# Expert units of 128 rows in a mixture-of-experts stage: rows stationary, gate and up columns moving in one product, hidden values turned by TensorE, down product one group later

## The chip, the cores and the metric

The program runs on one core of one Trainium2 chip. The metric is the device time of one execution in microseconds (us), lower is better. The kernel is a two-block transformer; the change touches one part of it, the expert stage, which takes some 17% of the time.

## What is computed

The reference has many stages; only the expert feed-forward matters here. 512 tokens with 1024 features each pick 2 of 8 experts, and each expert runs a SwiGLU with 3584 hidden columns on the rows that picked it:

```python
top_logits, top_idx = lax.top_k(logits, TOP_K)
...
order = jnp.argsort(flat_e)
group_sizes = jnp.bincount(flat_e, length=N_EXPERTS).astype(jnp.int32)
xs = xt[order // TOP_K]
hid = (jax.nn.silu(lax.ragged_dot(xs, w_gate, group_sizes))
       * lax.ragged_dot(xs, w_up, group_sizes))
ys = lax.ragged_dot(hid, w_down, group_sizes)
```

All of it is in float32. The weights of one expert (gate, up and down, 1024 x 3584 each) do not fit on the chip with everything else, so they are streamed from memory, and every unit of rows streams all of its expert's weights.

## The kernel before

`experts_stage` works through units. A unit is one expert's rows: at most 128 rows (units A, `ExpertRows` size 0) or at most 152 (units B, size 1). With these inputs there are five units A, then three units B. The 3584 hidden columns are cut into 14 groups of 256 (`GROUP`), and two sets of weight tiles alternate (index `b`, the group's parity). A float32 product of TensorE stands in the trace as two passes (two MATMUL rows, each with its own weight load), so the counts of the trace are twice those of the code.

In a unit A, for each group TensorE runs `first_half` (L1893): twice (`j`, 128 hidden columns each) `gate_up` (L1885), which takes 8 blocks of gate weights as stationary operand with the 128 turned rows `xu` moving, then 8 blocks of up weights. That gives gate and up values with hidden columns on the partitions, in banks 4 and 5 (gate), 6 and 7 (up). ScalarE applies Silu (L1983) to `gs`, VectorE multiplies (L2013) into `hid`. Then `down_a` (L1898) multiplies `hid` (stationary, 128 x 128, two of them) by the down weights (moving, 512 columns) and adds into banks 0 and 1, which hold the unit's output rows. In what follows P(g) is the gate and up product of group g and D(g) its down product. The order on TensorE before is P(0) D(0) P(1) D(1) ... P(13), the turning of the next unit's rows (`turn`, L1815, 8 transposes), D(13).

The weights come by DMAs that SyncE issues in a fixed order, for each group: wait until the gate and up tiles of this parity are free (`freed[b]`), issue gate (L1868) and up (L1869), wait until the down tile of this parity is free (`down_freed[b]`), issue down (L1875). 1 MiB each. `freed[b]` is incremented by the first matmul of D(g), `down_freed[b]` by the last one of D(g). P(g) waits for `loaded[b]`, that is for both gate and up. All three go through SyncE's one queue.

At the end of a unit VectorE copies the output from banks 0 and 1 (L2030), ScalarE's queue stores it (L1831), and GpSimd fetches the rows of the unit after the next one's turn (L1799 the indices, L1803 the rows, 512 KB).

Of the kernel before, what the change touches and what calls it, by code (L numbers as in the profile page):

```python
# [14 lines left out]
F32 = mybir.dt.float32  # L15
# [3 lines left out]
ALU = mybir.AluOpType  # L19
ACT = mybir.ActivationFunctionType  # L20
AX = mybir.AxisListType

P = 128
# [3 lines left out]
KD = D // P  # L27
# [7 lines left out]
GROUP = 256  # L35
# [125 lines left out]
class Stages:  # L161
# [10 lines left out]
    def sig(self, name, pool_dma=False):  # L172

        if name not in self.signals:
            self.signals[name] = Signal(self.nc, self.stack, name, True) if pool_dma else self.spare.pop()
        return self.signals[name]
# [11 lines left out]
def settle(eng, passed):  # L188


    eng.sem_inc(passed.sem, 1)
# [1573 lines left out]
class ExpertRows:  # L1765


    def __init__(self, S, R, size, st):
        self.S, self.R = S, R
        self.unfetched = 1 if size == 0 else 0  # L1770
        self.rows, self.row0 = UNIT_ROWS[size], FIRST_ROW[size]
        self.subs = [(r0, min(P, self.rows - r0)) for r0 in range(0, self.rows, P)]
        self.bank0 = (2, 4)[size]
        n = len(self.subs)
        self.xg = S.sb(f"rows{size}_x", [P, n, D], F32, st)
        self.xu = S.sb(f"rows{size}_xt", [P, KD, self.rows], F32, st)
        self.yrow = S.sb(f"rows{size}_y", [P, n, D], F32, st)
        self.index = S.sb(f"rows{size}_index", [P, n], I32, st)
        self.indexed, self.gathered = (S.sig(f"e{size}_{x}", pool_dma=True) for x in ("indexed", "gathered"))
        self.turned, self.stored, self.x_ready = (S.sig(f"e{size}_{x}") for x in ("turned", "stored", "x_ready"))  # L1780
        sig = lambda x: S.sig(f"s{size}_{x}")
        self.loaded, self.freed = [sig("loaded0"), sig("loaded1")], [sig("freed0"), sig("freed1")]
        self.down_loaded, self.down_freed = [sig("down_loaded0"), sig("down_loaded1")], [sig("down_freed0"), sig("down_freed1")]
        self.hidden, self.gate_up, self.gated = ([sig(x + "0"), sig(x + "1")] for x in ("hidden", "gate_up", "gated"))
        self.y_taken = sig("y_taken")
        if size:
            self.y_ready, self.y_turned, self.emitted = sig("y_ready"), sig("y_turned"), sig("emitted")

    def units(self, eng):
        size = 0 if self.row0 == 0 else 1  # L1790
# [43 lines left out]
def experts_stage(S, R, router, xn):  # L1834
    nc, a, ps = S.nc, S.a, S.ps
    n_groups = E_FF // GROUP
    per = n_groups // 2
    zeros = S.sig("s1_zeros")
    last = n_groups - 1
    with ExitStack() as st:  # L1840
        wg = S.sb("experts_wg", [P, 2, KD, GROUP], F32, st)
        wu = S.sb("experts_wu", [P, 2, KD, GROUP], F32, st)
        wd = S.sb("experts_wd", [P, 2, 2, D], F32, st)
        gs = S.sb("experts_gs", [P, 2, UNIT_ROWS[1]], F32, st)
        hid = S.sb("experts_hid", [P, 2, UNIT_ROWS[1]], F32, st)
        yT = S.sb("experts_yt", [P, KD, UNIT_ROWS[1]], F32, st)
        zero = S.sb("experts_zero", [P, BANK], BF16, st)
        A, B = ExpertRows(S, R, 0, st), ExpertRows(S, R, 1, st)
# [3 lines left out]
        with nc.Block("experts") as block:  # L1852
# [32 lines left out]
            def _(pe):  # L1885
# [8 lines left out]
                def first_half(E, b, u, i, n):  # L1894
                    pe.wait_ge(E.loaded[b].sem, E.loaded[b].at((u * per + i + 1) * 32))
                    gate_up(E, b, n, 0)
                    gate_up(E, b, n, 1)

                def down_a(b, u, i, n, first=False, final=False):
                    for j in range(2):  # L1900
                        pe.wait_ge(A.hidden[j].sem, A.hidden[j].at(n + 1))
                        if first and j == 0:
                            pe.wait_ge(A.y_taken.sem, A.y_taken.at(u))
                        if j == 0:
                            pe.wait_ge(A.down_loaded[b].sem, A.down_loaded[b].at((u * per + i + 1) * 16))
                        for hf in range(2):
                            ins = nc.tensor.matmul(ps[hf][:, :], hid[:, j, 0:P], wd[:, b, j, hf * 512:(hf + 1) * 512],  # L1907
                                                   start=(first and j == 0), stop=(final and j == 1), skip_group_check=True)
                            if j == 0 and hf == 0:
                                ins.then_inc(A.freed[b].sem, 1)  # L1910
                    ins.then_inc(A.down_freed[b].sem, 1)

                def down_b(b, u, i, n):
# [14 lines left out]
                n_a, n_b = A.units(pe), B.units(pe)  # L1928
                router.first_unit(pe, xn, A.bank0, A.turned)
                with pe.Fori(0, n_a) as u:  # L1930
                    pe.wait_ge(A.x_ready.sem, A.x_ready.at(2 * u + 2))
                    settle(pe, S.sig("passed_pe"))
                    n0 = u * n_groups
                    first_half(A, 0, u, 0, n0)
                    down_a(0, u, 0, n0, first=True)
                    with pe.Fori(0, per - 1) as i:
                        first_half(A, 1, u, i, n0 + i * 2 + 1)
                        down_a(1, u, i, n0 + i * 2 + 1)
                        first_half(A, 0, u, i + 1, n0 + i * 2 + 2)
                        down_a(0, u, i + 1, n0 + i * 2 + 2)  # L1940
                    first_half(A, 1, u, per - 1, n0 + last)
                    A.turn(pe, u + 1)
                    down_a(1, u, per - 1, n0 + last, final=True)
                B.turn(pe, 0)
                pe.wait_ge(A.y_taken.sem, A.y_taken.at(n_a))
                pe.wait_ge(A.x_ready.sem, A.x_ready.at(2 * n_a + 2))
# [2 lines left out]
                with pe.Fori(0, n_b) as u:  # L1949
                    pe.wait_ge(B.x_ready.sem, B.x_ready.at(4 * u + 4))  # L1950
                    settle(pe, S.sig("passed_pe"))
                    n0 = u * n_groups
# [24 lines left out]
            @block.scalar  # L1977
            def _(act):
                def silu(E, u, g, j):
                    n = u * n_groups + g  # L1980
                    act.wait_ge(E.gate_up[j].sem, E.gate_up[j].at(n + 1))
                    act.wait_ge(E.hidden[j].sem, E.hidden[j].at(n))
                    nc.scalar.activation(gs[:, j, 0:E.rows], ps[4 + j][:, 0:E.rows], ACT.Silu).then_inc(E.gated[j].sem, 1)  # L1983

                router.weigh(act)
                act.wait_ge(routed.sem, routed.at(2))
                n_a, n_b = A.units(act), B.units(act)
                with act.Fori(0, n_a) as u:
                    for g in range(n_groups):
                        silu(A, u, g, 0)  # L1990
                        silu(A, u, g, 1)
                    act.wait_ge(A.y_taken.sem, A.y_taken.at(u + 1))
                    settle(act, S.sig("passed_act"))
                    A.store(act, u)
                act.wait_ge(A.hidden[0].sem, A.hidden[0].at(n_a * n_groups))
                act.wait_ge(A.hidden[1].sem, A.hidden[1].at(n_a * n_groups))
                settle(act, S.sig("passed_act"))
                with act.Fori(0, n_b) as u:
                    for g in range(n_groups):
                        silu(B, u, g, 0)  # L2000
                        silu(B, u, g, 1)
                    act.wait_ge(B.emitted.sem, B.emitted.at(4 * u + 4))
                    settle(act, S.sig("passed_act"))
                    B.store(act, u)
                act.wait_ge(A.stored.sem, A.stored.at(16 * n_a))
                act.wait_ge(B.stored.sem, B.stored.at(32 * n_b))
                settle(act, S.sig("passed_act"))

            @block.vector
            def _(dve):  # L2010
                def hidden(E, u, g, j):
                    dve.wait_ge(E.gated[j].sem, E.gated[j].at(u * n_groups + g + 1))
                    nc.vector.tensor_tensor(hid[:, j, 0:E.rows], gs[:, j, 0:E.rows], ps[6 + j][:, 0:E.rows],  # L2013
                                            ALU.mult).then_inc(E.hidden[j].sem, 1)
# [4 lines left out]
                n_a, n_b = A.units(dve), B.units(dve)  # L2019
                A.place(dve, 0)  # L2020
                with dve.Fori(0, n_a) as u:
                    for g in range(n_groups):
                        hidden(A, u, g, 0)
                        hidden(A, u, g, 1)
                    A.place(dve, u + 1)
                    dve.wait_ge(A.down_freed[1].sem, A.down_freed[1].at(u * per + per))
                    dve.wait_ge(A.stored.sem, A.stored.at(16 * u))
                    settle(dve, S.sig("passed_dve"))
                    for hf in range(2):
                        ins = nc.vector.tensor_copy(A.yrow[:, 0, hf * 512:(hf + 1) * 512], ps[hf][:, :])  # L2030
                    ins.then_inc(A.y_taken.sem, 1)
# [1759 lines left out]
```

## Time and profile before

| | |
|---|---|
| median of 3 runs | 4344.17 us (4343.14 to 4347.41) |
| the profiled execution | 4342.29 us |
| its span in the profile | 4340.6 us |
| TensorE busy over the whole span | 3774.5 us (87%) |
| stage of units A | about 1303 to 2071 us |
| stage of units B | about 2071 to 2610 us |

PE is TensorE's matmuls and PEld its weight loads, DVE is VectorE, ACT ScalarE, POOL GpSimd; SPq, ACTq and POOLq are what these engines issue, DMAs among it. Times are from the span's start. A row of the timeline merges instructions of one line that follow each other; the length of a merged row includes the tail of its last matmul, so the distance between the starts of two rows tells what the first one costs TensorE.

### The profile page before, as it was taken

The numbers are of one execution on the slowest core, as the hardware profiler recorded it, in microseconds if no ns is written. First come the engines' busy times: TensorE is split into PE (matmuls) and PEld (weight loads), VectorE is DVE, ScalarE is ACT, GpSimd is POOL, SyncE is SP. The second block draws the span as 40 slices with busy tenths as digits, with TensorE's granted clock in tenths as the row PEclk, the third lists the DMA queues.
The fourth block names the chain that finished last, engine by engine and source line by source line (L and its number), as shares of the span: only waits on it lengthen the run. The fifth ranks groups of instructions, "written<-read, shape, count | busy, mean of one in ns | idle before, by whom it ended". The sixth has DMA issues, their size and how long they took to land. (4 is left out here: it accounts for less than half of the span.)

```text
span 4340.6 us, 45502 instructions
## 1 busy us (share of the span) xinstructions
PE 3774.5 (87%) x17099; PEld 2506.2 (58%) x17106; DVE 1706.2 (39%) x3683; ACT 626.4 (14%) x1566; POOL 1094.1 (25%) x1162
## 2 busy tenths in 40 slices
PE   7989999998988999999999996998766767766666
PEld 3455777744747888888999993465422322222222
DVE  2052231013730000000000004748888776877655
ACT  1121000013520000000000003143211111111011
POOL 0010000001500000000000000003667777777775
PEclk9989999999989999999999998989888888888888
DMA  3143675330018889888777764036899999999998
GB/s 114 48 152 122 240 246 191 105 136 1 20 59 267 307 294 311 306 306 298 264 248 256 252 223 140 25 103 234 336 390 387 419 416 420 413 418 415 420 414 354
DMA packets 549127, 1092.57 MB, mean 252 GB/s; under 512 B 37577, under 2 KB 336982, under 8 KB 548870
## 3 DMA queue, kind: packets, MB, share of 16 engines
q1 hardware_dynamic: 395802, 539.66, 36.8%
q0 software_dynamic: 150768, 546.25, 31.3%
q10 hardware_dynamic: 2428, 5.03, 0.3%
q8 instruction: 69, 1.13, 0.1%
q14 instruction: 60, 0.49, 0.0%
HBM read 1069.55 MB, written 21.30 MB: 251 GB/s over the span
## 5 line engine op out<-in xcount | busy, mean ns | idle before, releaser
L3223 PE MATMUL banks<-peer_ring,consts 128*128 128x512 f32 x1512 | 844.7, 719 | 375.9 <-DMA peer_ring<-in_peer_v_dram,peer_expert 375.9
L3223 PEld LDWEIGHTS banks<-peer_ring,consts 128*128 128x128 f32 x1512 | 338.1, 231 | 877.2 <-DMA peer_ring<-in_peer_v_dram,peer_expert 469.4
L3424 DVE SCALAR_TENSOR_TENSOR peer_ring<-peer_ring,banks 128x1024 f32<-128x1024 f32 x512 | 594.0, 1216 | 253.2 <-DMA peer_ring<-in_peer_u_dram,peer_expert 252.2
L3127 POOL DMA_INDIRECT peer_ring<-in_peer_u_dram,peer_expert x512 | 483.7, 945 | 547.6 <-POOLq L2744 348.0
L3127 POOL DMA_INDIRECT peer_ring<-in_peer_v_dram,peer_expert x512 | 487.4, 952 | 173.5 <-issue 138.5
L2013 DVE TENSOR_TENSOR experts_hid<-experts_gs,banks 128x128 f32<-128x128 f32 (+1 forms) x224 | 66.5, 297 | 1175.8 <-ACT experts_gs L1983 1175.8
L1890 PEld LDWEIGHTS banks<-rows_xt,experts_wg 128*128 128x128 f32 x3584 | 447.0, 192 | 45.2 <-issue 44.9
L1890 PE MATMUL banks<-rows_xt,experts_wg 128*128 128x128 f32 (+1 forms) x3584 | 462.4, 283 | 11.4 <-DMA experts_wu<-in_moe_w_up_dram 9.4
L1890 PE MATMUL banks<-rows_xt,experts_wu 128*128 128x128 f32 (+1 forms) x3584 | 461.1, 282 | 0.0
L1890 PEld LDWEIGHTS banks<-rows_xt,experts_wu 128*128 128x128 f32 x3584 | 441.0, 192 | 0.0
L405 PE MATMUL banks<-xT,proj_w 128*128 128x512 f32 (+1 forms) x720 | 319.3, 601 | 9.0 <-PEq L3575 5.5
L1799 POOL DMA_DIRECT2D rows_index<-token_of_row x13 | 7.4, 575 | 1060.3 <-PE banks L1815 1042.4
L1907 PE MATMUL banks<-experts_wd,experts_hid 128*128 128x512 f32 x560 | 251.9, 593 | 0.0
L405 PEld LDWEIGHTS banks<-xT,proj_w 128*128 128x128 f32 (+1 forms) x720 | 135.6, 191 | 185.3 <-issue 184.0
L1023 POOL TENSOR_TENSOR hgrn_both<-k,hgrn_diff 128x256 f32<-128x256 f32 x56 | 44.3, 815 | 775.6 <-ACT hgrn_diff L934 761.2
L1983 ACT ACTIVATE experts_gs<-banks 128x128 f32<-128x128 f32 (+1 forms) x224 | 63.7, 285 | 1183.0 <-PE banks L1890 1183.0
L3455 DVE SCALAR_TENSOR_TENSOR banks<-peer_ring,peer_wgt,banks 128x1024 f32<-128x1024 f32 x130 | 167.3, 1287 | 80.5 <-DMA peer_ring<-in_peer_v_dram,peer_expert 80.1
L1920 PE MATMUL banks<-experts_hid,experts_wd 128*128 128x152 f32 x1344 | 180.5, 293 | 0.0
L1920 PEld LDWEIGHTS banks<-experts_hid,experts_wd 128*128 128x128 f32 x1344 | 176.4, 190 | 0.4
L408 PE MATMUL banks<-proj_w,xT 128*128 128x512 f32 (+1 forms) x448 | 174.1, 549 | 0.0
L1357 PE MATMUL banks<-xT,ffn_wg 128*128 128x256 f32 x704 | 161.2, 383 | 1.2 <-ACT ada_c L1395 1.2
L1431 DVE TENSOR_TENSOR ffn_hid<-ffn_gs,banks 128x256 f32<-128x256 f32 x44 | 18.5, 421 | 360.7 <-ACT ffn_gs L1401 360.7
(506 smaller groups left out, 3757.6 us busy)
## 6 DMA issues: line engine op xcount, KB each, us to landing
experts_wg<-in_moe_w_gate_dram SPq DMA_DIRECT2D x112, 1024.0 KB, 5.1
experts_wu<-in_moe_w_up_dram SPq DMA_DIRECT2D x112, 1024.0 KB, 7.7
experts_wd<-in_moe_w_down_dram SPq DMA_DIRECT2D x112, 1024.0 KB, 8.1
ada_w<-in_w_ada_dram SPq DMA_DIRECT2D x12, 2048.0 KB, 8.0
ffn_wg<-in_ffn_w_gate_dram SPq DMA_DIRECT2D x22, 1024.0 KB, 7.8
ffn_wu<-in_ffn_w_up_dram SPq DMA_DIRECT2D x22, 1024.0 KB, 10.4
ffn_wd<-in_ffn_w_down_dram SPq DMA_DIRECT2D x22, 1024.0 KB, 11.8
y_rows<-blank SPq DMA_DIRECT2D x1, 12288.0 KB, 42.2
```

Source lines behind the costliest of these rows:

```text
L405: last = nc.tensor.matmul(out_of(g), wk[:, m * P:m * P + width], xT[:, k, :], start=(k == 0), stop=(k == KD - 1))
L408: last = nc.tensor.matmul(out_of(g), xT[:, k, m * P:(m + 1) * P], wk[:, 0:n], start=(k == 0), stop=(k == KD - 1))
L1357: last = nc.tensor.matmul(ps[bank][:, 0:ROWS], w[:, b, k, j * P:(j + 1) * P], xT[:, k, u * ROWS:(u + 1) * ROWS], start=(k == 0), stop=(k = ...
L1890: ins = nc.tensor.matmul(ps[bank][:, 0:E.rows], w[:, b, k, j * P:(j + 1) * P], E.xu[:, k, :], start=(k == 0), stop=(k == KD - 1))
L1907: ins = nc.tensor.matmul(ps[hf][:, :], hid[:, j, 0:P], wd[:, b, j, hf * 512:(hf + 1) * 512], start=(first and j == 0), stop=(final and j = ...
L1920: ins = nc.tensor.matmul(ps[d // 2][:, at:at + B.rows], wd[:, b, j, d * P:(d + 1) * P], hid[:, j, :], start=False, stop=False, skip_group_ ...
L1983: nc.scalar.activation(gs[:, j, 0:E.rows], ps[4 + j][:, 0:E.rows], ACT.Silu).then_inc(E.gated[j].sem, 1)
L2013: nc.vector.tensor_tensor(hid[:, j, 0:E.rows], gs[:, j, 0:E.rows], ps[6 + j][:, 0:E.rows], ALU.mult).then_inc(E.hidden[j].sem, 1)
L3127: pool.indirect_dma_start(out=ring[:, slot_of(kind, n, b), :], out_offset=None, in_=tables[kind == "value"], in_offset=bass.IndirectOffset ...
L3223: last = nc.tensor.matmul(ps[bank + hf][:, :], diag[:, n % 2 * B + b, :], ring[:, slot_of("value", n, b), hf * 512:(hf + 1) * 512], start= ...
L3424: nc.vector.scalar_tensor_tensor(row, row, 1.0, rows_at, ALU.mult, ALU.mult, accum_out=acts[:, t % 2, at:at + 1]).then_inc(dotted[q].sem, 1)
L3455: ins = nc.vector.scalar_tensor_tensor(sum_at, row, weight(n, b), sum_at, ALU.mult, ALU.add)
```

## The change

For units A only:

- the gate and up tiles become one tile `w_in` with the 256 gate columns and the 256 up columns of a block side by side; the two DMAs stay, each writing its half of every 2 KB line;
- P(g) is now 8 products with the rows `xu` stationary and 512 columns of `w_in` moving, into one bank (4 or 5, by parity): gate in its first half, up in the second, with rows on the partitions;
- ScalarE's Silu and VectorE's multiplication are one instruction each of 256 columns, to new tiles `a_gs` and `a_rows`;
- `turn_hidden` turns `a_rows` by two TensorE transposes into bank 6, in the middle of the next group's product, and ScalarE copies them to `hid`;
- D(g) comes after P(g+1);
- `freed` of a group is incremented by the first matmul of the down product that follows its P, which is now D of the group before (for group 0 by the first matmul of P(1)); `down_freed` still by the last matmul of its own D.

```diff
-        wg = S.sb("experts_wg", [P, 2, KD, GROUP], F32, st)
-        wu = S.sb("experts_wu", [P, 2, KD, GROUP], F32, st)
+        w_in = S.sb("experts_w", [P, 2, KD, 2 * GROUP], F32, st)
+        wg, wu = w_in[:, :, :, 0:GROUP], w_in[:, :, :, GROUP:2 * GROUP]
...
-                def down_a(b, u, i, n, first=False, final=False):
+                def products_a(b, n, ks, frees=None):
+                    for k in ks:
+                        ins = nc.tensor.matmul(ps[4 + b][:, :], A.xu[:, k, :], w_in[:, b, k, :], start=(k == 0), stop=(k == KD - 1))
+                        if k == 0 and frees is not None:
+                            ins.then_inc(A.freed[frees].sem, 1)
+                    if ks[-1] == KD - 1:
+                        ins.then_inc(A.gate_up[b].sem, 1)
+
+                def turn_hidden(b, n):
+                    pe.wait_ge(A.hidden[b].sem, A.hidden[b].at(n + 1))
                     for j in range(2):
-                        pe.wait_ge(A.hidden[j].sem, A.hidden[j].at(n + 1))
...
+                        ins = nc.tensor.transpose(ps[6][:, j * P:(j + 1) * P], a_rows[:, j * P:(j + 1) * P], S.const("ident"))
+                    ins.then_inc(A.hid_turned.sem, 1)
...
+                def next_group(b, u, i, before, first=False):
+                    pe.wait_ge(A.loaded[b].sem, A.loaded[b].at((u * per + i + 1) * 32))
+                    pe.wait_ge(A.hidden[b].sem, A.hidden[b].at(u * per + i))
+                    products_a(b, u * per + i, range(KD // 2), frees=0 if first else None)
+                    turn_hidden(1 - b, u * per + before)
+                    products_a(b, u * per + i, range(KD // 2, KD))
+
+                def down_a(b, u, i, first=False, final=False):
+                    pe.wait_ge(A.hid_copied.sem, A.hid_copied.at(u * n_groups + i * 2 + b + 1))
+                    if first:
+                        pe.wait_ge(A.y_taken.sem, A.y_taken.at(u))
+                    pe.wait_ge(A.down_loaded[b].sem, A.down_loaded[b].at((u * per + i + 1) * 16))
+                    for j in range(2):
                         for hf in range(2):
                             ins = nc.tensor.matmul(ps[hf][:, :], hid[:, j, 0:P], wd[:, b, j, hf * 512:(hf + 1) * 512],
                                                    start=(first and j == 0), stop=(final and j == 1), skip_group_check=True)
-                            if j == 0 and hf == 0:
-                                ins.then_inc(A.freed[b].sem, 1)
+                            if j == 0 and hf == 0 and not final:
+                                ins.then_inc(A.freed[1 - b].sem, 1)
                     ins.then_inc(A.down_freed[b].sem, 1)
...
-                    n0 = u * n_groups
-                    first_half(A, 0, u, 0, n0)
-                    down_a(0, u, 0, n0, first=True)
+                    first_group(u)
+                    next_group(1, u, 0, 0, first=True)
+                    down_a(0, u, 0, first=True)
                     with pe.Fori(0, per - 1) as i:
-                        first_half(A, 1, u, i, n0 + i * 2 + 1)
-                        down_a(1, u, i, n0 + i * 2 + 1)
-                        first_half(A, 0, u, i + 1, n0 + i * 2 + 2)
-                        down_a(0, u, i + 1, n0 + i * 2 + 2)
-                    first_half(A, 1, u, per - 1, n0 + last)
+                        next_group(0, u, i + 1, i)
+                        down_a(1, u, i)
+                        next_group(1, u, i + 1, i + 1)
+                        down_a(0, u, i + 1)
+                    turn_hidden(1, u * per + per - 1)
                     A.turn(pe, u + 1)
-                    down_a(1, u, per - 1, n0 + last, final=True)
+                    down_a(1, u, per - 1, final=True)
...
-                        silu(A, u, g, 0)
-                        silu(A, u, g, 1)
+                        act.wait_ge(A.gate_up[g % 2].sem, A.gate_up[g % 2].at(u * per + g // 2 + 1))
+                        nc.scalar.activation(a_gs[:, :], ps[4 + g % 2][:, 0:GROUP], ACT.Silu).then_inc(A.gated[g % 2].sem, 1)
+                        act.wait_ge(A.hid_turned.sem, A.hid_turned.at(u * n_groups + g + 1))
+                        nc.scalar.activation(hid[:, :, 0:P], ps[6][:, 0:GROUP].rearrange("p (j r) -> p j r", j=2),
+                                             ACT.Copy).then_inc(A.hid_copied.sem, 1)
...
-                        hidden(A, u, g, 0)
-                        hidden(A, u, g, 1)
+                        dve.wait_ge(A.gated[g % 2].sem, A.gated[g % 2].at(u * per + g // 2 + 1))
+                        nc.vector.tensor_tensor(a_rows[:, :], a_gs[:, :], ps[4 + g % 2][:, GROUP:2 * GROUP],
+                                                ALU.mult).then_inc(A.hidden[g % 2].sem, 1)
```

SyncE's code is unchanged. On TensorE, the first three groups of a unit A stand before as follows (L1890 is P, half of it per pair of rows, L1907 is D; the first two D here are D(0) and D(1)):

```order
L1890 MATMUL banks<-rows_xt,experts_wg 128x128 x8
L1890 MATMUL banks<-rows_xt,experts_wu 128x128 x8
L1887 REGISTER_ALU
L1890 MATMUL banks<-rows_xt,experts_wg 128x128 x8
L1890 MATMUL banks<-rows_xt,experts_wu 128x128 x8
L1901 REGISTER_ALU
L1903 REGISTER_ALU
L1905 ISA
L1907 MATMUL banks<-experts_wd,experts_hid 128x512 x2
L1901 REGISTER_ALU
L1907 MATMUL banks<-experts_wd,experts_hid 128x512 x2
```

In the changed kernel the same place reads (L1905 is P, L1914 the two transposes of the hidden values, L1936 is D):

```order
L1905 MATMUL banks<-experts_w,rows_xt 128x512 x8
L1924 REGISTER_ALU
L1905 MATMUL banks<-experts_w,rows_xt 128x512 x4
L1912 REGISTER_ALU
L1914 MATMUL banks<-consts,experts_a_rows 128x128 x2
L1905 MATMUL banks<-experts_w,rows_xt 128x512 x4
L1930 ISA
L1932 REGISTER_ALU
L1933 ISA
L1936 MATMUL banks<-experts_wd,experts_hid 128x512 x4
```

32 products of 128 columns have become 8 of 512, and D(0) has moved behind the whole of P(1), with the transposes in P(1)'s middle.

On ScalarE a unit A starts in the changed kernel with these rows, where before there were two Silu of 128 columns for each group and nothing between:

```order
L2020 ACT_TABLE_LOAD
L2020 ACTIVATE experts_a_gs<-banks 128x256
L2021 ISA
L2022 ACTIVATE experts_hid<-banks 128x2x128
L2019 REGISTER_ALU
L2020 ACTIVATE experts_a_gs<-banks 128x256
```

A copy stands between each two Silu, and the table load still stands once at the head of the unit.

## Rows read from the trace of the kernel before

**Rows 1.** Stretches: busy us per engine, granted TensorE clock, DMA share, GB/s.

```profile
core 0: us, PE busy (x) PEld busy (x) DVE busy (x) ACT busy (x) POOL busy (x), PEclk, DMA share, GB/s
1303.00:1345.00 42.00, 30.70 (x203) 27.78 (x204) 4.85 (x18) 2.39 (x5) 9.49 (x10) 0.81 0.98 236
1345.00:2071.00 726.00, 726.00 (x4943) 594.87 (x4942) 50.23 (x154) 42.80 (x140) 9.23 (x12) 1.00 0.88 302
```

**Rows 2.** Timeline of a group of unit A: start, length, engine, line, operation.

```profile
1503.66 3.60 PE L1907 MATMUL banks<-experts_wd,experts_hid 128*128 128x512 f32 x8
1503.87 0.28 ACT L1983 ACTIVATE experts_gs<-banks 128x128 f32<-128x128 f32 x1 [3.22 <-PE banks L1890]
1504.17 0.29 DVE L2013 TENSOR_TENSOR experts_hid<-experts_gs,banks 128x128 f32<-128x128 f32 x1 [3.21 <-ACT experts_gs L1983]
...
1507.10 1.95 PE L1890 MATMUL banks<-rows_xt,experts_wg 128*128 128x128 f32 x16
...
1508.88 1.95 PE L1890 MATMUL banks<-rows_xt,experts_wu 128*128 128x128 f32 x16
...
1514.24 3.60 PE L1907 MATMUL banks<-experts_wd,experts_hid 128*128 128x512 f32 x8
...
1517.68 1.95 PE L1890 MATMUL banks<-rows_xt,experts_wg 128*128 128x128 f32 x16
```

**Rows 3.** Timeline of SyncE's queue: the DMA issues around the same group.

```profile
1504.94 0.38 SPq L1868 DMA_DIRECT2D experts_wg<-in_moe_w_gate_dram  x1
1505.41 0.53 SPq L1869 DMA_DIRECT2D experts_wu<-in_moe_w_up_dram  x1
1507.49 0.37 SPq L1875 DMA_DIRECT2D experts_wd<-in_moe_w_down_dram  x1
1515.51 0.37 SPq L1868 DMA_DIRECT2D experts_wg<-in_moe_w_gate_dram  x1
```

**Rows 4.** DMA issues from 1500 to 1560: median us from issue to landing.

```profile
experts_wg<-in_moe_w_gate_dram SPq DMA_DIRECT2D x6, 1024.0 KB, 5.1
experts_wu<-in_moe_w_up_dram SPq DMA_DIRECT2D x6, 1024.0 KB, 7.6
experts_wd<-in_moe_w_down_dram SPq DMA_DIRECT2D x5, 1024.0 KB, 8.1
```

**Rows 5.** Timeline of the turning at a unit's end and what follows it.

```profile
1471.05 1.04 PE L1815 MATMUL banks<-consts,rows_x 128*128 128x128 f32 x8
...
1471.92 3.60 PE L1907 MATMUL banks<-experts_wd,experts_hid 128*128 128x512 f32 x8
...
1473.18 0.37 SPq L1868 DMA_DIRECT2D experts_wg<-in_moe_w_gate_dram  x1
...
1475.36 1.95 PE L1890 MATMUL banks<-rows_xt,experts_wg 128*128 128x128 f32 x16
...
1476.55 0.98 POOL L1803 DMA_INDIRECT rows_x<-xn_rows,rows_index  x1 [3.14 <-DMA rows_index<-token_of_row]
...
1477.32 0.40 ACTq L1831 DMA_DIRECT2D y_rows<-rows_y  x1
```

**Rows 6.** DMA issues from 1473 to 1474, at that unit's end: us to landing.

```profile
experts_wg<-in_moe_w_gate_dram SPq DMA_DIRECT2D x1, 1024.0 KB, 6.0
experts_wu<-in_moe_w_up_dram SPq DMA_DIRECT2D x1, 1024.0 KB, 9.7
```

**Rows 7.** Timeline of the first unit's start.

```profile
1307.23 4.22 SPq L1869 DMA_DIRECT2D experts_wu<-in_moe_w_up_dram  x1
...
1322.54 3.60 PE L1907 MATMUL banks<-experts_wd,experts_hid 128*128 128x512 f32 x8
...
1323.82 0.38 SPq L1868 DMA_DIRECT2D experts_wg<-in_moe_w_gate_dram  x1
...
1334.41 3.78 PE L1890 MATMUL banks<-rows_xt,experts_wg 128*128 128x128 f32 x16 [8.27 <-DMA experts_wu<-in_moe_w_up_dram]
1337.98 2.70 PE L1890 MATMUL banks<-rows_xt,experts_wu 128*128 128x128 f32 x16
...
1340.52 1.95 PE L1890 MATMUL banks<-rows_xt,experts_wg 128*128 128x128 f32 x16
```

**Rows 8.** DMA issues from 1307 to 1308: the up load that P(1) of the first unit waits for.

```profile
experts_wu<-in_moe_w_up_dram SPq DMA_DIRECT2D x1, 1024.0 KB, 27.0
```

**Rows 9.** Instructions by line and form, another stage: 256 columns on ScalarE and VectorE.

```profile
L1431 DVE TENSOR_TENSOR ffn_hid<-ffn_gs,banks 128x256 f32<-128x256 f32 x44 | 18.5, 421 | 360.7 <-ACT ffn_gs L1401 360.7
L1401 ACT ACTIVATE ffn_gs<-banks 128x256 f32<-128x256 f32 x44 | 16.9, 383 | 434.1 <-PE banks L1357 434.1
```

**Rows 10.** DMA issues from 1240 to 1290, each into an empty queue.

```profile
xn_rows<-mix SPq DMA_DIRECT2D x3, 512.0 KB, 2.6
```

More of the change, by code:

```diff
@@ L1787, in __init__ @@
             self.y_ready, self.y_turned, self.emitted = sig("y_ready"), sig("y_turned"), sig("emitted")
+        else:
+            self.hid_turned, self.hid_copied = sig("hid_turned"), sig("hid_copied")
     def units(self, eng):
@@ L1840, in experts_stage @@
     with ExitStack() as st:
-        wg = S.sb("experts_wg", [P, 2, KD, GROUP], F32, st)
-        wu = S.sb("experts_wu", [P, 2, KD, GROUP], F32, st)
+        w_in = S.sb("experts_w", [P, 2, KD, 2 * GROUP], F32, st)
+        wg, wu = w_in[:, :, :, 0:GROUP], w_in[:, :, :, GROUP:2 * GROUP]
         wd = S.sb("experts_wd", [P, 2, 2, D], F32, st)
         gs = S.sb("experts_gs", [P, 2, UNIT_ROWS[1]], F32, st)
+        a_gs = S.sb("experts_a_gs", [P, GROUP], F32, st)
+        a_rows = S.sb("experts_a_rows", [P, GROUP], F32, st)
         hid = S.sb("experts_hid", [P, 2, UNIT_ROWS[1]], F32, st)
@@ L1897, in first_half @@
                     gate_up(E, b, n, 1)
-                def down_a(b, u, i, n, first=False, final=False):
-                    for j in range(2):
-                        pe.wait_ge(A.hidden[j].sem, A.hidden[j].at(n + 1))
[L1902 to L1905, printed above, removed]
+                def products_a(b, n, ks, frees=None):
[5 more added lines that the diff above has]
+                        ins.then_inc(A.gate_up[b].sem, 1)
@@ new lines, in turn_hidden, with first_group @@
+                def turn_hidden(b, n):
+                    pe.wait_ge(A.hidden[b].sem, A.hidden[b].at(n + 1))
+                    for j in range(2):
+                        ins = nc.tensor.transpose(ps[6][:, j * P:(j + 1) * P], a_rows[:, j * P:(j + 1) * P], S.const("ident"))
+                    ins.then_inc(A.hid_turned.sem, 1)
+                def first_group(u):
+                    pe.wait_ge(A.loaded[0].sem, A.loaded[0].at((u * per + 1) * 32))
+                    pe.wait_ge(A.hidden[0].sem, A.hidden[0].at(u * per))
+                    products_a(0, u * per, range(KD))
@@ L1994, in _ @@
                     A.store(act, u)
-                act.wait_ge(A.hidden[0].sem, A.hidden[0].at(n_a * n_groups))
-                act.wait_ge(A.hidden[1].sem, A.hidden[1].at(n_a * n_groups))
-                settle(act, S.sig("passed_act"))
                 with act.Fori(0, n_b) as u:
```

## The prediction

> **What bounds the kernel now.** Read the stretches first [rows 1]: from 1345 to 2071 us, where all but the first two groups of the units A lie, TensorE is busy in all of the 726 us, at a granted clock of 1.00 (2.4 GHz). So TensorE's own work sets the pace there. The DMA share beside it is 0.88: little air. The timeline of one group [rows 2] gives the unit of account: P from 1507.10 to 1514.24 is 7.14 us, D from 1503.66 to 1507.10 is 3.44, and the next P starts 10.58 after the last. The reader should then see how full the DMA queue is in these 10.58 us. SyncE issues gate and up at 1504.94 and 1505.41 (just after D's first matmul) and down at 1507.49 (0.39 after the next P has begun, once D has ended) [rows 3]; they land 5.1, 7.6 and 8.1 later [rows 4], the last at 1515.59. From the first issue to the last landing a set of three takes **W = 10.65 us**, as long as a group. It hurts nobody now, because gate and up land at 1513.0 and are wanted at 1517.68, when P(g+2) starts: 4.6 us of slack.
>
> **TensorE's own work: 2.8 us less.** P was 32 products of two passes, 64 passes in 7.14 us, 0.112 each for 128 columns. It becomes 8 products of 512 columns, 16 passes. D is of that very form (128 x 512 moving, 8 passes in 3.44 us), so a pass costs 0.43 and P 16 x 0.43 = 6.88. The array streams as many columns as before; only the small cost for each pass goes. The turning adds two transposes; eight cost 1471.05 to 1471.92, 0.87 us [rows 5], so two cost 0.22. A group is 6.88 + 0.22 + 3.44 = 10.54 instead of 10.58. Over 5 x 14 groups: 70 x 0.04 = -2.8 us.
>
> Beside this row stands a rule that says much more. In the Trainium skill, the page "TensorE: Matmul & The Clock Gate" (section "Back-to-back issue gap") gives for sustained streams of weight load and matmul about 81 ns at 128 columns and 131 ns at 512. By those figures the wide P would take about 0.4 of the old one. The trace disagrees: 0.112 against 0.43, a factor of 3.8 for four times the columns.
>
> **ScalarE and VectorE: hidden.** ScalarE starts 0.21 after P's end and VectorE 0.30 after ScalarE [rows 2]. With 256 columns they take 0.38 and 0.42 [rows 9], so the product of both is there 0.21 + 0.38 + 0.42 + about 0.1 = 1.1 us after P's end. The transposes want it half a P (3.44 us) after. The copy back (0.38, some 0.7 with both hand-overs) has the other 3.44 us; at a unit's end it has the 0.87 of the turning. So nothing, with 0.2 us to spare at the tightest place. Were the table loaded anew for each function (1.3 us), only the unit's end would show it, 1.1 us five times.
>
> **The DMAs: the real price, 21 us.** Both release points stay where they were in code, but D has moved. The order is now P(n-1) D(n-2) P(n) D(n-1) P(n+1). SyncE's queue is strict: down(n), gate(n+1), up(n+1). Down(n) waits for D(n-2)'s last matmul. Gate and up(n+1) have been free since that D's first matmul, but they stand behind down(n) in the queue. So all three go out together 0.39 us after D(n-2) ends, and the last of them, up(n+1), is wanted at P(n+1), only 10.54 us after that end. They land W later and TensorE takes about 0.2 to start (up(1) of the first unit, issued at 1307.23, lands 27.0 later at 1334.2, and P(1) starts at 1334.41 [rows 7, 8]). That makes 0.39 + 10.65 + 0.2 = 11.24, which is 0.70 too late. A P that starts 0.70 late gives the next set 0.70 more, so the following P is in time: every second P waits. In a unit these are P(3), P(5) to P(13), six; P(2) has a set that was issued earlier. 5 x 6 x 0.70 = **+21.0 us**. W is the term that matters: a tenth of a us of W is 3 us of the result. The nearest row is the same three transfers in another order, 10.65, and I take it. Lower bound: 512 KB in lines of 4 KB, meeting an empty queue, land after 2.6 us [rows 10]; less half of down's 2.5 us (8.1 + 1507.49 against 7.6 + 1505.41) that is 1.3 of fixed cost, where gate has 5.1 less about 3 = 2.1. Down now opens the set, and with 1.3 W is 9.85. But that row is a store and far from this one. Upper bound: three transfers at gate's and up's 3 us each, 11.2.
>
> A page weighs in for the lower end: "DMA: Bandwidth & Descriptors" of the Trainium skill (section "Anatomy of one DMA — SWDGE (gpsimd) path") fits 2.0 us plus bytes / 436 GB/s, for another issuing path. By it 3.15 MB would take 9.2 us and no P would wait; the trace's 10.65 speaks against it.
>
> **Unit ends: 8 us.** Four times a unit A follows another. There the fetch of rows and the store of the output, 512 KB each, share the DMA engines: issued at 1476.55 and 1477.32, with P(0) at 1475.36 [rows 5]. Up, issued with gate at 1473.18, then takes 9.7 instead of 7.6 [rows 4, 6], 2.1 more. Now up(1) of the new unit goes out with the set at the end of D(12). P(1) is ready after 0.22 + 0.87 + 3.44 + 6.88 = 11.41; the set lands at 0.39 + 10.65 + 2.1 to 2.3 + 0.2 = 13.4. Wait 2.0, four times: **+8.1 us**. At least 0.8 less each with the small W, at most 0.9 more if both transfers, 1 MB at 2.5 to 3 us, go wholly ahead of up(1). Before, D(0) stood between and up had slack.
>
> **The first unit: 3.4 us.** P(1) waits 8.27 us for up(1), whose load is slow there (27.0) and is issued before any change [rows 7, 8]. Before, P(0) and D(0) were done by then; now only P(0). D(0)'s 3.44 us no longer fills the wait: +3.4. The slow clock after the wait (3.57 + 2.54 us for what is 3.57 at full clock, 0.81 granted over the stretch [rows 1]) stays. Gate and up(2), now issued after 1334.41 instead of at 1323.82, have until about 1347: no wait.
>
> Units B keep their order and products; the weight tile's other layout costs them nothing that a row shows.
>
> **Sum.** -2.8 + 21.0 + 8.1 + 3.4 = +29.7 us. The profiled execution took 4342.3 (span 4340.6, 1.7 outside), so 4372.0; the median of the runs is 1.9 higher, so 4373.9. Take 4374.
>
> **Rivals.** (A) No steady waits: W under 10.0, because a set that starts with down's long lines gets going sooner. For it: rows 10. Against: W is measured with the same bytes, and a queue that is never empty inside the set. It leaves -2.8 + 3.4 and at most 4 x 1.2 at the unit ends: +1 to +6, 4345 to 4350, no measurable change. The point from which it decides is 0.39 + W + 0.2 = 10.54; between W = 9.95 and 10.65 lie 4350 to 4374.
> (B) The half lines of 1 KB at a step of 2 KB make gate and up slower to write. At W = 11.2 the 30 waits are 1.25: 37.5 + 4 x 2.6 + 0.6 = +48, 4393; beyond that it grows by 3 us a tenth. No row shows such a destination.
> (C) The wide product is much cheaper than D's passes, the page's case. P at 0.4 of 7.14 gives a TensorE period of 6.5; the set's law (two periods = TensorE's work + 11.24) gives 8.9 a group, 70 x -1.7 + 11 = -108, about 4236. Two passes of the same form in D at 0.43 speak against it; this is the faster side.
>
> **Chances.** Forecast, W from 10.2 to 11.2: 0.72, from 4359 to 4393. (A), with W below 10.2: 0.17. (B) beyond 4393: 0.07. Faster by (C) or something unseen: 0.04. The range 4350 to 4393 leaves out half of (A), (B) and (C), near 0.2. A measurement of this kernel tells about 0.2% (8.7 us) from no change. Within it (up to 4352.9) lies about two thirds of (A), 0.11; slower 0.85; faster 0.04.
>
> **What would show it.** In the new profile: P's 16 passes at 0.43 and D unchanged; PE idle before L1905, released by a DMA to `experts_w`, some 30 times about 0.7 us and 4 times about 2 us, next to one wait of about 12 us; SyncE's three issues in one burst after each D. Wrong if those waits are missing (W was too large), if L1914 or L1936 waits for DVE or ACT, or if a P lasts other than 6.9 + 0.2.

## The result, and the profile of the changed kernel

| | before | changed |
|---|---|---|
| median of the runs | 4343.66 us | 4391.55 us (4389.35 to 4403.33) |
| the profiled execution | 4342.29 us | 4403.33 us |
| ratio | | 1.0117 [1.0105, 1.0129] |

The changed kernel is 47.9 us slower; 30 had been forecast. The units A, the only ones whose code differs, take 759.65 us of the 4340.6 before, some 17%; with the units B the expert stage is some 30%. The profiled execution is the slowest of its four, 61 us above the profile of before. Start, as there, with the stretches of the units A.

```profile
core 0: us, PE busy (x) PEld busy (x) DVE busy (x) ACT busy (x) POOL busy (x), PEclk, DMA share, GB/s
1303.00:1345.00 42.00, 25.40 (x97) 16.07 (x98) 5.09 (x20) 2.05 (x3) 9.48 (x10) 0.76 0.89 195
1345.00:2071.00 726.00, 690.63 (x1686) 303.03 (x1685) 37.27 (x80) 53.97 (x131) 9.23 (x12) 0.99 0.84 281
```

Where TensorE had been busy in all of 726 us [rows 1], 35 us are now idle. The waits of TensorE between 1290 and 2300 us (engine, tile and line, what it waited for: total, times, longest) name one cause for them:

```profile
PE banks L1905 <- DMA experts_w<-in_moe_w_up_dram: 50.2, 38, 12.3
```

L1905 is P, and each wait is for the up load. The timeline shows one of them, against the group ahead of it which did not wait [rows 2 has the group of before]:

```profile
1509.59 3.60 PE L1905 MATMUL banks<-experts_w,rows_xt 128*128 128x512 f32 x8
1509.98 0.37 SPq L1879 DMA_DIRECT2D experts_wd<-in_moe_w_down_dram  x1
1510.75 0.37 SPq L1872 DMA_DIRECT2D experts_w<-in_moe_w_gate_dram  x1
1511.22 0.53 SPq L1873 DMA_DIRECT2D experts_w<-in_moe_w_up_dram  x1
1513.02 0.38 PE L1914 MATMUL banks<-consts,experts_a_rows 128*128 128x128 f32 x2
...
1516.67 3.60 PE L1936 MATMUL banks<-experts_wd,experts_hid 128*128 128x512 f32 x8
...
1520.48 0.37 SPq L1879 DMA_DIRECT2D experts_wd<-in_moe_w_down_dram  x1
1521.08 3.69 PE L1905 MATMUL banks<-experts_w,rows_xt 128*128 128x512 f32 x8 [0.81 <-DMA experts_w<-in_moe_w_up_dram]
1521.64 0.38 SPq L1872 DMA_DIRECT2D experts_w<-in_moe_w_gate_dram  x1
```

SyncE issues down, gate and up in one burst, 0.39 us after the product before has ended, where before gate had gone out 2.2 us and up 1.7 us ahead of that end [rows 3]. D starts at 1516.67 and takes 3.43; the next P starts 1.0 us after D is through. (The profile's 0.81 counts from the end of the last matmul's tail, so each wait costs 0.17 more than it says.) ACT and DVE are not named for L1914 or L1936: the turned values are always there. The landings in the same stage, to be read against the 5.1, 7.6 and 8.1 of before [rows 4] (DMA issues, 1345 to 2120 us):

```profile
experts_wd<-in_moe_w_down_dram SPq DMA_DIRECT2D x68, 1024.0 KB, 5.0
experts_w<-in_moe_w_gate_dram SPq DMA_DIRECT2D x68, 1024.0 KB, 7.3
experts_w<-in_moe_w_up_dram SPq DMA_DIRECT2D x68, 1024.0 KB, 9.7
```

One more thing the prediction did not have. After four of the 38 waits, beside the long one of the first unit, the first half of P lasts much longer, here at the start of the second unit:

```profile
1488.17 7.03 PE L1905 MATMUL banks<-experts_w,rows_xt 128*128 128x512 f32 x16
1497.27 5.39 PE L1905 MATMUL banks<-experts_w,rows_xt 128*128 128x512 f32 x8 [2.06 <-DMA experts_w<-in_moe_w_up_dram]
1502.50 0.38 PE L1914 MATMUL banks<-consts,experts_a_rows 128*128 128x128 f32 x2
```

and the granted clock of that half, beside that of the half after the 0.81 us wait, is

```profile
1497.30:1502.50 5.20, 5.20 (x9) 2.13 (x10) 0.00 (x0) 0.00 (x0) 0.00 (x0) 0.67 0.93 339
1521.10:1524.60 3.50, 3.50 (x8) 1.55 (x9) 0.00 (x0) 0.00 (x0) 0.00 (x0) 1.00 0.82 281
```

so part of it ran at 1.2 GHz: 5.2 us for work of 3.4. (Of this half, 1497.3 to 1501.3 shows 0.56 to 0.59, and 1501.3 to 1502.5 a granted clock of 1.00.)

### The profile page after: what moved, and what is told of

Same layout as the page of the kernel before. It is cut to its first block and busy times, and to the rows that moved or that the text cites. A ratio compares the mean times of both kernels' runs of the same rounds, so it can differ in the third digit from the quotient of the medians.

```text
span 4401.6 us, 38712 instructions
## 1 busy us (share of the span) xinstructions
PE 3800.5 (86%) x13879; PEld 2231.4 (51%) x13886; DVE 1697.2 (39%) x3613; ACT 641.6 (15%) x1566; POOL 1096.3 (25%) x1162
## 3 DMA queue, kind: packets, MB, share of 16 engines
q1 hardware_dynamic: 395802, 539.66, 36.6%
## 5 line engine op out<-in xcount | busy, mean ns | idle before, releaser
L1905 PE MATMUL banks<-experts_w,rows_xt 128*128 128x512 f32 x1120 | 516.8, 606 | 50.5 <-DMA experts_w<-in_moe_w_up_dram 50.2
L1905 PEld LDWEIGHTS banks<-experts_w,rows_xt 128*128 128x128 f32 x1120 | 206.8, 193 | 309.0 <-issue 308.8
L1894 PE MATMUL banks<-rows_xt,experts_w 128*128 128x152 f32 x2688 | 356.0, 294 | 2.0 <-DVE rows_xt L1828 2.0
L1894 PEld LDWEIGHTS banks<-rows_xt,experts_w 128*128 128x128 f32 x2688 | 351.4, 191 | 2.3 <-issue 2.1
L2053 DVE TENSOR_TENSOR experts_a_rows<-experts_a_gs,banks 128x256 f32<-128x256 f32 x70 | 29.5, 421 | 741.0 <-ACT experts_a_gs L2020 741.0
L1936 PE MATMUL banks<-experts_wd,experts_hid 128*128 128x512 f32 x560 | 251.8, 592 | 0.0
L2042 DVE TENSOR_TENSOR experts_hid<-experts_gs,banks 128x152 f32<-128x152 f32 x84 | 26.3, 313 | 485.9 <-ACT experts_gs L2012 485.9
L1936 PEld LDWEIGHTS banks<-experts_wd,experts_hid 128*128 128x128 f32 x560 | 106.0, 190 | 131.5 <-issue 131.5
## 6 DMA issues: line engine op xcount, KB each, us to landing
ffn_wu<-in_ffn_w_up_dram SPq DMA_DIRECT2D x22, 1024.0 KB, 10.5
ffn_wd<-in_ffn_w_down_dram SPq DMA_DIRECT2D x22, 1024.0 KB, 11.8
```

The source lines that it names most:

```text
L1894: ins = nc.tensor.matmul(ps[bank][:, 0:E.rows], w[:, b, k, j * P:(j + 1) * P], E.xu[:, k, :], start=(k == 0), stop=(k == KD - 1))
L1905: ins = nc.tensor.matmul(ps[4 + b][:, :], A.xu[:, k, :], w_in[:, b, k, :], start=(k == 0), stop=(k == KD - 1))
```

## Experiments

**Theory S** is the prediction's: gate and up of the next group but one stand in SyncE's queue behind down, which waits for the end of D; with D a group later, that set lands too late. Rival **P**: the wide product, its transposes and its restarts lose the time in TensorE itself. Rival **Q**: the DMA engines are too busy, in any order. The W of the expectations is the time from the set's first issue to its last landing. In them `in` stands for gate and up together. A time is the median of the run's executions, and "before" that of the same call.

### Gate and up ahead of down

```diff
-for each group g: in(g), down(g)
+in(0); then for each group g: in(g+1), down(g)
```

(This and the next diffs of SyncE's order are in short form; the waits that belong to each load move with it.)

> The changed kernel with one edit in SyncE's order for units A: gate and up of group n+1 are issued ahead of down of group n, so they no longer stand behind a load that waits for the end of D(n-2). Theory S (the set of three loads, released at D's end and wanted one group later, sets the pace): gate and up go out at the first matmul of D(n-2), about 14 us before P(n+1), and land in about 8.1; the 34 waits for them go, the slow clock after them too, and in the first unit up(1) no longer follows down(0), so P(1) starts some 4 us sooner. TensorE's own 10.52 us per group against 10.58 is then all that is left: 4335 to 4345 us. Rival P (the wide product, its transposes and the restarts cost TensorE itself the time): the waits may go but the stage stays long, 4365 us or more. Rival Q (the DMA engines are simply too busy in this stage, in any order): waits of about 1 us stay, 4375 us or more.

Measured 4339.98 us against 4345.7, ratio 0.9988 [0.9979, 0.9997]. All the steady waits are gone; in the list of waits two for a load are left, 6.1 us at P(1) of the first unit (at 1329.88) and 0.6 us at 1935.97. The timeline of a group reads

```profile
1501.26 3.60 PE L1933 MATMUL banks<-experts_w,rows_xt 128*128 128x512 f32 x8
1504.69 0.38 PE L1942 MATMUL banks<-consts,experts_a_rows 128*128 128x128 f32 x2
1504.91 3.60 PE L1933 MATMUL banks<-experts_w,rows_xt 128*128 128x512 f32 x8
1508.35 3.60 PE L1964 MATMUL banks<-experts_wd,experts_hid 128*128 128x512 f32 x8
1511.78 3.60 PE L1933 MATMUL banks<-experts_w,rows_xt 128*128 128x512 f32 x8
```

10.52 us from P to P, without a gap, with the DMA share at 0.89 (before 0.88). P and Q fall: the new products and the same bytes fit. This version is 0.1% below the kernel before: its group is shorter by 0.06 us, and in the first unit P(1) starts 13.2 us after P(0) (1316.66 to 1329.88), where it was 19.1, since up(1) no longer follows down(0). Of these 5.9 us 2.5 are gained; the other 3.4 are D(0), which before was done by then and is now still to come.

### Late, but ahead

e1 changes two things at once, when gate and up are issued and what stands ahead of them. Here only the second:

```diff
-for each group g: in(g), down(g)
+in(0); then for each group g: wait for the end of D(g-2), in(g+1), down(g)
```

> The changed kernel; for units A SyncE holds gate and up of group n+1 back until D(n-2) has ended, as late as in the changed kernel, but then issues them ahead of down(n). It parts the two halves of theory S: the release at D's end, and the place behind down's load. My reading: the place decides. Up lands 0.7 + 0.47 + 7.7 = 8.9 us after D's end plus 0.2, against 10.52: no steady waits, none at the unit ends either (2.1 more is 11.2 against 11.4), and the first unit as in e1: 4337 to 4346 us. If the late release decided, the waits would stay near 1 us: 4370 or more.

Measured 4339.86 against 4344.13, 0.9993 [0.9983, 1.0002]. In the timeline of SyncE's queue gate leaves 0.7 us after D's end (P starts at 1513.71), and no longer ahead of it. In the changed kernel it left 1.2 us after it, behind down's issue (1510.75 against 1509.59):

```profile
1514.38 0.37 SPq L1891 DMA_DIRECT2D experts_w<-in_moe_w_gate_dram  x1
1514.86 0.52 SPq L1892 DMA_DIRECT2D experts_w<-in_moe_w_up_dram  x1
1515.64 1.12 SPq L1896 DMA_DIRECT2D experts_wd<-in_moe_w_down_dram  x1
```

and it lands 5.2 us later, up 7.7, and down 9.4 (1500 to 1800 us). Up is there 8.8 us after D's end (1522.52 against 1513.71) and is wanted after 10.5; the half us by which the changed kernel releases it later would still fit. Three waits for a load are left, 5.3 us in the first unit and 1.1 and 2.0 us later. So the late release alone costs next to nothing; the 1 MB ahead in the queue does. The set of three takes 1.26 + 9.4 = 10.7 us in this order, which is the forecast's W.

### The kernel before, with down first

```diff
-for each group g: in(g), down(g)
+for each group g: down(g), in(g)
```

> The kernel before, its products and TensorE's order untouched; for units A SyncE issues down of a group ahead of gate and up of the same group. So gate and up wait for D's end, as in the changed kernel, and are wanted 10.58 us after it. Theory S: the set lands 0.39 + 10.95 + 0.2 = 11.5 us after D's end, every second P waits about 1 us, more at the unit ends, and the first P starts 3 to 5 us later: 4375 to 4395 us, as slow as the changed kernel though no product was changed. Rivals P and Q: nothing in TensorE's work or in the bytes has changed, 4340 to 4350 us.

Measured 4413.14 against 4345.7, 1.0157 [1.0141, 1.0172], +67 us. No product of the change is in it, and still TensorE waits 37 times for up, 58.1 us in all, 8.3 and 4.4 of them in the first unit. So the order of the loads alone makes a loss of this kind. It lies 18 us beyond the expected range: each unit end has a wait of 3 to 4.7 us (3.06, 4.12, 4.21, 4.71), where the changed kernel has 2.1 to 2.4 in its two profiles. The loads land 5.1, 7.5 and 9.9 us after their issues (1345 to 2071 us), as late as in the changed kernel, though they go to the old tiles.

### The size of the down load

The changed kernel with half of each down load left out, and with 512 KB added behind it:

```diff
-dv = dn[bass.ds((i * 2 + b) * GROUP, GROUP), :].rearrange("(j p) d -> p j d", p=P)
-sp.dma_start(wd[:, b, :, :], dv).then_inc(E.down_loaded[b].sem, 16)
+dv = dn[bass.ds((i * 2 + b) * GROUP, P), :]
+sp.dma_start(wd[:, b, 0, :], dv).then_inc(A.down_loaded[b].sem, 16)
```

> The changed kernel with half of each down load left out for units A (512 KB instead of 1 MB; both halves of D use the half that is loaded, so the sums are others). SyncE's order stays. Theory S: W falls by 1.3 us, from 10.95 and 11.8 (the two parities) to 9.65 and 10.5, the landing from 11.5 and 12.4 to 10.2 and 11.1 after D's end against 10.52 that TensorE needs: half of the steady waits go and the rest are about 0.6; with the unit ends and the first unit some 4355 to 4368 us. Rival P: unchanged, 4385 to 4395. Rival Q: also faster, so this run does not part S from Q.

Measured 4382.62 against 4345.7, 1.0080 [1.0065, 1.0096]: 9 us off the changed kernel instead of 24 to 37. The waits hardly shrank: without the first two groups, 35 waits of 31.8 us, 0.91 each, where the changed kernel has 36 of 36.6 us, and 40 of 34.2 in a second profile (below). Why is in the landings (1345 to 2071 us):

```profile
experts_w<-in_moe_w_gate_dram SPq DMA_DIRECT2D x65, 1024.0 KB, 7.0
experts_w<-in_moe_w_up_dram SPq DMA_DIRECT2D x65, 1024.0 KB, 9.5
experts_wd<-in_moe_w_down_dram SPq DMA_DIRECT2D x65, 512.0 KB, 3.6
```

Down lands 1.4 us sooner (3.6 for 5.0), gate and up only 0.2 to 0.3. The traffic of one set, whose down is issued at 1534.50, gate at 1535.64 and up at 1536.11, shows where the time goes (columns as in the stretches above, the last two DMA share and GB/s):

```profile
1536.00:1537.00 1.00, 1.00 (x3) 0.41 (x3) 0.00 (x0) 0.00 (x0) 0.00 (x0) 1.00 0.91 360
1537.00:1538.00 1.00, 1.00 (x5) 0.55 (x4) 0.00 (x0) 0.03 (x1) 0.00 (x0) 1.00 0.37 100
1538.00:1539.00 1.00, 1.00 (x3) 0.38 (x2) 0.00 (x0) 0.35 (x1) 0.00 (x0) 1.00 0.74 221
1539.00:1540.00 1.00, 1.00 (x4) 0.46 (x3) 0.00 (x0) 0.00 (x0) 0.00 (x0) 1.00 1.01 338
```

Down's 512 KB are in by 1537.99, but gate's data come in full only some 3 us after gate's issue, so the DMA engines stand partly idle between the two: half the bytes leave a hole instead of an earlier landing. Why gate's data start so late is not shown. The rest of what went was in the first unit (waits of 9.4 for 12.3) and in the slow halves: one is left outside the first unit.

> The changed kernel with 512 KB more loaded behind each down load of units A, into a tile that nothing reads; D waits for it too. Theory S: W grows by 1.3 us, each of the 34 waits by as much (every second P waits, so about half of W's growth per group): +40 to +48 us against the changed kernel, 4432 to 4440 us. If W grew the period one for one (every P waits), it would be +90. Rival P: below +10.

The edit:

```diff
+spare = S.sb("experts_spare", [P, 2, D], F32, st)
...
 sp.dma_start(wd[:, b, :, :], dv).then_inc(A.down_loaded[b].sem, 16)
+sp.dma_start(spare[:, b, :], dn[bass.ds((i * 2 + b) * GROUP, P), :]).then_inc(A.down_loaded[b].sem, 16)
```

Measured 4453.63 against 4345.7, 1.0248 [1.0232, 1.0264]: +62 us on the changed kernel against 44 expected. 40 waits, 95.8 us; nearly every second P waits, mostly 1.7 to 2.2 us, the unit ends 4.5 to 5.8, and nine halves of P run slow, the first unit's among them. Bytes that are added ahead of gate count in full (the sets' median W is 12.4 us, 1.3 more), bytes that are taken away hardly.

### Only the starts

```diff
-for each group g: in(g), down(g)
+in(0), in(1), down(0), down(1); then for each g from 2: in(g), down(g)
```

> The changed kernel; SyncE issues gate and up of groups 0 and 1 of each unit of A before its first down, and from then on in the changed kernel's order (down(n), then gate and up(n+1)). Theory S: only the unit ends and the first unit are mended: about 6 us at the first unit (up(1) no longer behind down(0): e1 had P(1) start 6 us sooner), 9.5 us of waits in P(1) of the four later units and about 5 us of slow clock and restarts after them: 20 us off the changed kernel, 4368 to 4376 us. The steady waits, some 30 of about 1 us, stay. A rival, that one common cause sits in the start, would take most of the waits away: below 4355.

Measured 4374.88 against 4345.67, 1.0066 [1.0051, 1.0082]: 16.7 us off the changed kernel, within the expectation. P(1) of the first unit waits 6.6 us for 12.3, the unit ends do not wait, no half after them is slow; 31 waits stay, 0.9 us each on the mean (33.6 in all with the first unit's). The steady waits and those of the starts are separate, as the theory has it.

### Down at once

```diff
-first_group; next_group(1), down_a(0), ... (in short form: D(g) behind P(g+1), transposes in P's middle)
+P(g), turn_hidden(g), D(g) for each g, freed[b] by D(g)'s first matmul
```

> The changed kernel without the shift by a group: P(g) in one piece, the two transposes, then D(g) at once; gate and up are freed by D(g)'s own first matmul, as before the change. Theory S: the loads have their old time again (4.6 us to spare), so no P waits for a DMA beyond the first unit; instead TensorE waits twice in each group, about 1.1 us for Silu and product and 0.7 us for the copy: 70 x 1.8 = +126 us, 4465 to 4480 us. Rival P (the wide product and its transposes lose the time themselves): the same waits and the P's own loss on top, above 4500. It tells what the shift is worth.

Measured 4471.27 against 4345.67, 1.0287 [1.0269, 1.0306]. The loads keep time; TensorE waits for the other engines (waits, 1290 to 2300 us):

```profile
PE banks L1914 <- DVE experts_a_rows L2046: 65.1, 70, 0.9
PE banks L1930 <- ACT experts_hid L2015: 36.5, 65, 0.6
```

A group takes 12.49 us, 1.9 more than before. Against e1, which keeps the shift and has its loads in time, it is 131 us: that is what the shift by a group is worth to the wide form, and it can't simply be taken back.

### The order of e1 in the kernel before

```diff
-for each group g: in(g), down(g)
+in(0); then for each group g: in(g+1), down(g)
```

> The kernel before, products and TensorE's order untouched, with SyncE's order of e1 for units A (gate and up of group n+1 ahead of down of group n). It asks whether e1's 5.5 us below the kernel before come from the loads' order alone. If so: 4336 to 4342 us here too. My reading: not. Down(0) then lands late in the first unit, where the loads are slow, and here D(0) comes before P(1), so TensorE waits in D(0) for what it waited for in P(1) before: 4342 to 4349, the same as before within 0.1%. The gain then belongs to the products' form and to the shift, which lets P(1) start without down(0).

Measured 4464.21 against 4345.67, 1.0268 [1.0254, 1.0282]: +118.5 us, and the expectation was plainly wrong. I had looked at the first unit only. Here D(g) comes right behind P(g), and down(g), behind in(g+1), goes out only after D(g-1) has started:

```profile
1526.18 3.60 PE L1935 MATMUL banks<-experts_wd,experts_hid 128*128 128x512 f32 x8
...
1538.18 3.70 PE L1935 MATMUL banks<-experts_wd,experts_hid 128*128 128x512 f32 x8 [1.25 <-DMA experts_wd<-in_moe_w_down_dram]
```

gate at 1527.49, down at 1528.81, down's landing 9.4 later at 1538.2, D at once after it. 12.0 to 12.2 us a group, for nearly every group (62 waits for down, 103.4 us in all), since nothing gives the lost time back in the next one: 70 x 1.4 and the starts. The same law in another place: a load that stands behind two others is wanted before the three can land. The order of e1 needs D a group later, and the changed kernel's D a group later needs the order of e1.

### SyncE's loop written out

```diff
-with sp.Fori(0, per) as i:
+for i in range(per):
```

> The changed kernel with SyncE's loop over a unit's groups written out, same order, same waits. In the changed kernel down's issue to gate's issue is 0.77 us, but 1.16 where the loop's branch lies between, and there the set takes 11.8 us instead of 10.95. Theory: the branch is the cause of that 0.85 us; without it all sets take about 10.95, the waits fall from about 1.03 to 0.8 us on the mean, about 6 to 12 us off: 4378 to 4386 us. Rival: the late landing is not the branch's (an uneven start of the DMA engines), and the time stays at 4388 to 4394.

Measured 4388.55 against 4345.67, 1.0094 [1.0079, 1.0110]: only 3 us off the changed kernel, above the theory's range and at the lower end of the rival's. Down to gate is now 0.63 us, and up lands 1.09 + 10.0 = 11.1 us after down's issue. Taken set by set from issues and landings (1345 to 2060 us), the median W is 11.1 us in both kernels; a quarter of the sets are at 11.8 or more with the loop (11.6 in the second profile, below), at 11.2 or more without. So the branch has its part in the longest sets, but that W is above 10.7 with down first is not its doing.

### The changed kernel again

> The changed kernel once more, unedited, for a second profile of it: do the size of the steady waits, the waits of P(1) at the four unit ends and the slow clock after some of them repeat? Theory S: 4386 to 4396 us, 34 to 38 waits of 46 to 52 us in all, each P(1) at a unit's end about 2 us; how many are followed by a slow clock I leave open (4 in the first profile).

4390.31 against 4344.13, 1.0111 [1.0094, 1.0127]. Four of the five executions took 4388.82 to 4395.52 us; the profiled one took 16113.55, for no reason that the runs show, and its profile says nothing of this kernel. One more profile answers the question:

> The changed kernel, unedited, for one more profile, since its first one is of an execution 12 us above the median of its runs. Theory: near 4391 us, the stage of units A about 803 us from its first product to units B's (it was 815), with fewer or no halves of P at the slow clock (7 us of the difference) and the same 34 to 38 waits, 44 to 50 us in all.

4394.22 against 4344.87, single executions. 42 waits of 49.6 us in all, one slow half after a wait of 2.4 us, instead of four. From the first P of units A to the first of units B it is 808.0 us, where the first profile had 815.0 and before 759.65. The waits repeat, the slow halves do not.

## Why the prediction was off

**The bound** (TensorE's own work, full DMA queue beside it): right. **TensorE's own work**: 10.52 us a group against 10.58 (e1's timeline); -4 us where -2.8 was forecast. A pass of 512 columns costs 0.43 in P as in D. By the sustained figures of "TensorE: Matmul & The Clock Gate" (section "Back-to-back issue gap") of the Trainium skill one would estimate that the wide form saves more than half of P. The trace disagrees (16 passes in 6.87 us, where 64 took 7.14), the measurement decides, and rival (C) is out. **ScalarE and VectorE**: hidden, no wait names them.

**The steady waits: the mechanism was right, its size was the step that failed.** The prediction put 30 x 0.70 = 21.0 us. The first profile has 32 waits of 27.8 us in the list (50.2 less 1.3 before the first P, 12.3 of the first unit and 8.8 at the unit ends). To each come the 0.17 of the tail and 0.10 for the half P after it (1521.08 to 1524.61 is 3.53, where 1509.59 to 1513.02 is 3.43): 27.8 + 32 x 0.27 = 36.4, or 1.14 each.

Under the 0.70 lies W, "the nearest row is the same three transfers in another order, 10.65, and I take it". In the other order it is not 10.65. Down first: 1.24 + 9.7 = 10.9 for the set of 1509.98, 1.63 + 10.3 = 11.9 for that of 1520.48 (landings from its own list), and 11.1 as the median of the stage's sets; gate first, also in one burst: 10.7 (e9). With 11.1 the prediction's own law gives 0.39 + 11.1 + 0.2 - 10.52 = 1.17 for a wait, against the measured 1.14. Its slope of 3 us for a tenth would have put the forecast at 4382 with W = 10.9 and at 4388 with 11.1. That W lies near the upper end of the range stated for it (10.2 to 11.2), and so the measured 4391.55 lies just inside the stated range; but of the 18 us by which the change cost more than the sum says, 13.5 are W's.

The ramp that rival (A) hoped for went the other way. Down alone, into an empty queue, lands after 5.0 to 5.1 us, as late as gate, though its 1 MB takes half a us less when it stands behind others; so the set loses that half us by having down at its head. In the longest sets a thin tail comes on top. In the set of 1520.48, which lands at 1532.38, the last full us before it carries almost nothing:

```profile
1530.00:1531.00 1.00, 1.00 (x4) 0.52 (x3) 0.00 (x0) 0.00 (x0) 0.00 (x0) 1.00 0.74 236
1531.00:1532.00 1.00, 0.86 (x3) 0.03 (x1) 0.00 (x0) 0.00 (x0) 0.00 (x0) 1.00 0.06 19
```

By the fit of "DMA: Bandwidth & Descriptors" (section "Anatomy of one DMA — SWDGE (gpsimd) path") of the Trainium skill, which is for another issuing path, the estimate for the set is 9.2 us; the shortest sets of the units A took 10.5 us (kernel before), and the measurement decides.

**Rival (B)**, slower writes to the half lines: out. In units B, which load into the new tile in the old order, the medians after are 5.1, 7.6 and 6.8 us, before 5.1, 7.7 and 6.8. In e9's units A, which load into it too, gate and up land after 5.2 and 7.7, before after 5.1 and 7.6.

**Unit ends**: forecast 8.1, measured 2.06, 2.25, 2.28 and 2.23, 9.9 with the 0.27 each. **First unit**: forecast 3.4, measured 12.27 - 8.27 = 4.0. Both near enough.

**The slow clock**: not in the sum at all. Four halves of 5.22 instead of 3.43 make 7 us in the first profile, one in the second 1.8. The prediction had noted a slow stretch only after the 8 us wait and not asked whether waits of 2 us could bring one.

Together -4 + 36.4 + 9.9 + 4.0 + 6.8 = 53 of the 55.3 us that the stage grew in the first profile. The rest of the 61 us lies outside the stage (1.3 ahead of it, 1.7 in units B, 2.8 behind), where the code is the same. The second profile, nearer to the median of the runs, has the same account: -4 + 35.0 (36 steady waits) + 10.0 + 5.0 + 1.7 = 48 of the 48.4 us that the stage grew.

What is shown: the loss is the order of the loads (e2 makes it without the change, e1 and e9 take it away with the change kept). What is open: why down at the head of a set starts half a us slower than gate, where the tail of the longest sets comes from, and why waits of the same length are followed by a slow clock in some cases and not in others.

## What to carry to other kernels

When a step is moved behind another, write down for each load in the same queue when it is released, what stands ahead of it and when it is wanted, before counting instructions: here one load of 1 MB that waits for a later point stood ahead of two that were free. Held back alone, those two were still in time (e9); behind its 1 MB they were not. A prefetch order and a compute order are one design; the order that repaired the changed kernel cost the old one 118 us. And where the slack comes out at less than the spread of a transfer time (here 11.2 against 10.5, with W unknown to 0.5), measure that time in its new order first, since each tenth of it counts by the number of waits.

## What the runs showed that was not expected

- A load of 1 MB in lines of 4 KB takes 5.0 us into an empty queue, where 1 MB in lines of 1 KB takes 5.1; behind others it adds 2.5 and the other 3.0.
- After waits of 1.9 to 2.3 us TensorE's granted clock was 0.67 over the next half P in four cases of the first profile, and one of 2.4 us in the second was followed by a half as long (5.23 us). Others of the same length, 2.23 us before the P at 1979.67 and 2.32 before that at 1361.91 in the first profile, were followed by a full clock.
- A wait that TensorE's list gives as 0.81 us costs 1.1 from P to P: 0.17 of tail that it doesn't count and 0.10 of restart.
